# A fused transformer kernel: the NSA attention of the first mixer stepped by head pair instead of by token tile

## The chip, the cores and the metric

One NeuronCore of a Trainium2 chip runs the whole program. The metric is device time in microseconds (us) from launch to end, as the median of several executions. One further execution was profiled; its span and its rows are used below.

## The reference

Two transformer layers on 256 tokens of width 1024. The first layer's mixer is what the change touches. It has eight NSA query heads in two key/value groups (heads of 64), each with a compressed, a selected and a windowed branch; with 256 tokens, all blocks are selected and the window covers everything, so both of the latter branches are plain causal attention. Beside them run four slots of dilated attention.

```python
def masked_softmax(s, mask):
    s = jnp.where(mask, s, NEG_INF)
    return jax.nn.softmax(s, axis=-1) * mask
...
        ps = masked_softmax(ss, kpos <= t[:, None])
        o_s = jnp.einsum('bghtm,bgtmd->btghd', ps.astype(vs.dtype), vs)
...
        pw = masked_softmax(sw, wmask)
        o_w = jnp.einsum('bghtk,bkgd->btghd', pw.astype(vw.dtype), vw)
        o = gt[..., 0:1] * o_c + gt[..., 1:2] * o_s + gt[..., 2:3] * o_w
...
def reference(x, norm_g, even_w_in, ...):
    h = x
    for layer in range(DEPTH):
        y = rmsnorm(h, norm_g[layer, 0])
        y = even_mixer(...) if layer % 2 == 0 else odd_mixer(...)
        h = h + rmsnorm(y, norm_g[layer, 1])
        y = conv_ffn(rmsnorm(h, norm_g[layer, 2]), ...)
        h = h + rmsnorm(y, norm_g[layer, 3])
    return h
```

## The kernel before

Each engine runs a stream that was written out by hand, and semaphores tie the streams together. The attention of the first mixer stands between its input projection (`in0`) and its output projection (`out0`). It is a list of 16 items, `ITEMS`. Items 0 to 7 are dilated: one head slot and one token tile each, with 512 score columns. Items 8 to 15 are NSA: `("nsa", j, t)` is the head pair j (one head of each group) and the token tile t. The even items have t = 1 and see 256 keys ("wide", 4 x 256 score columns, for two heads times two branches); the odd ones have t = 0 and see 128 keys ("narrow", 4 x 128). Items 8 and 9 are one head pair, 10 and 11 the next.

An item n goes through these steps:

1. TensorE: scores (`dil_qk` or `nsa_qk`, two groups of matmuls, the second adds the mask; signals `it_scores`).
2. VectorE: negated row maxima (`it_maxima`, signals `it_max`).
3. ScalarE: the exponentials with their sums (`it_probs`; one activation for a dilated item, four for an NSA item; signals `it_exp`).
4. VectorE: reciprocals of the sums (`it_coefs`), then the probabilities times the coefficient (`it_scale`, signals `it_scaled`). For an NSA item a small product with the gates lies between.
5. TensorE: turns the scaled probabilities with transposes (`it_turn`, four of 128x128, eight for a wide item; signals `it_turned`).
6. ScalarE copies the first 512 turned columns to SBUF (`it_turned_out`, signals `it_pT0`); VectorE copies the other 512 of a wide item (`it_pT1`).
7. TensorE: the product with the values (`dil_values`, `nsa_values`, signals `it_pv`). When both token tiles of a head pair are in, ScalarE and VectorE split the output into a high and a low part (`tile_hi`, `tile_lo`) as operands of `out0`.

Banks of PSUM hold the scores (0 to 3; an even NSA item has banks 0 and 1, an odd one banks 2 and 3), the turned probabilities (4, and 5 for the second half of a wide item) and the outputs (6 and 7 in turn, by tile). `nsa_qk(n)` waits for the exponentials of item n - 2 (`it_exp`), whose scores lie in its banks. `probs` and `probsT` have three buffers each. The loops on the engines are skewed: in step n, TensorE issues the scores of n + 2, turns n, and multiplies the values of n - 1; ScalarE copies out the turned n and then does the exponentials of n + 2; VectorE takes the maxima of n + 2 and scales n + 1. The last NSA values are mixed with the first blocks of `out0` (`out_blocks`). The weights of that stage's last unit are split in halves (`SPLIT_AT`).

Of the kernel before, what the change touches and what calls it, by code (L numbers as in the profile page):

```python
# [15 lines left out]
F32 = mybir.dt.float32  # L16
# [64 lines left out]
def build(nc, x, weights, wgate, cmpw2, pe2, gpre, gpost, convw, rope, ropec, cmask, rows, masks, gcol, tri,  # L81
          out):
    ctx = ExitStack()
    with ctx:
# [89 lines left out]
        psh = ps[:, :, :].rearrange("p b (q c) -> p (b q) c", c=SEQ)  # L174

# [99 lines left out]
        TILE_OUT = {5: 0, 9: 1, 11: 2, 13: 3, 15: 4}  # L275
# [10 lines left out]
        def s_half(n):  # L286

            return 4 * (n % 2)
# [65 lines left out]
        def coefs_until(n):  # L354
            return sum(1 if kind == "dil" else 2 for kind, _, _ in ITEMS[:n + 1])
# [44 lines left out]
        def _(act):  # L400
# [125 lines left out]
            def it_probs(n):  # L526
                kind, _, t = ITEMS[n]
                s, w, o, v = n % 3, P * (t + 1), s_half(n), n % 4
# [6 lines left out]
                else:  # L535
                    for m in range(4):
                        act.activation(probs[:, s, m * w:(m + 1) * w], psh[:, o + m, 0:w], ACT.Exp,
                                       bias=stat[:, v, m:m + 1], accum_out=stat[:, v, 4 + m:5 + m]).then_inc(it_exp, 1)

            def it_turned_out(n):  # L540
# [4 lines left out]
                act.copy(probsT[:, n % 3, 0:BLK], ps[:, 4, :]).then_inc(it_pT0, 1)  # L545

            def tile_hi(tile):
                act.wait_ge(it_pv, TILE_DONE[tile])
                if tile < NSA0:
                    act.copy(xhi[:, tile, :].rearrange("p (i r) -> p i r", r=RES),  # L550
                             in_order(ps[:, 6 + tile % 2, 0:SEQ])).then_inc(ot_hi, 1)
                else:
                    act.copy(xhi[:, tile, :], ps[:, 6 + tile % 2, 0:SEQ]).then_inc(ot_hi, 1)
# [72 lines left out]
            for n in range(NI + 2):  # L626
                if n == 2:
                    act.wait_ge(unit_used, EVEN_END["unit", 6])
                    act.wait_ge(residue_rstd, 16 * TT * RES)
                    values_out(V_DIL + 256, 6, 0, BLK, True)  # L630
                if n < NI:
                    it_turned_out(n)
                if n in TILE_OUT:
                    tile_hi(TILE_OUT[n])
                if n + 2 < NI:
                    it_probs(n + 2)
                if n == NI:
                    tile_hi(NT - 1)
                if n in SPLIT_AT:
                    k = SPLIT_AT.index(n)  # L640
                    split_half(FIRST_UNIT["out0"] + LOOK + k // 2, k % 2)
# [133 lines left out]
        def _(dve):  # L775
# [285 lines left out]
            def it_maxima(n):  # L1061
                kind, _, t = ITEMS[n]
                s, w, o = n % 4, P * (t + 1), s_half(n)
                dve.wait_ge(it_scores, n + 1)
                if kind == "dil":
                    dve.tensor_reduce(stat[:, s, 0:1], ps[:, n % 4, :], AX.X, ALU.max, negate=True).then_inc(it_max, 1)
                else:
                    dve.tensor_reduce(stat[:, s, 0:4], psh[:, o:o + 4, 0:w], AX.X, ALU.max,
# [1010 lines left out]
```

## Time and profile before

| | |
|---|---|
| median of 3 executions | 657.6 us (657.31 to 657.97) |
| span of the profiled execution | 655.8 us |
| TensorE matmul busy | 646.6 us (99%) |
| VectorE busy | 460.1 us (70%) |
| ScalarE busy | 385.1 us (59%) |
| granted TensorE clock, mean | 1.000 |
| chain that ended last | TensorE 93%, VectorE 2%, GpSimd 2%, ScalarE 1% |

The span runs from the first to the last instruction of the profiled execution; the device time has about 1.8 us more around it. Busy shares are over the whole program, of which the attention items are some 45 us (98 to 148 us). Matmuls overlap in their pipeline, so the start of a group of instructions to the start of the next is what a group takes, and not its own duration. L numbers are lines of the kernel before.

### The profile page before, as it was taken

Reading aid. Unit: us, or ns where it says so; the run is one execution under the profiler, and the core shown is the slowest. Engines: PE = TensorE matmul, PEld = TensorE weight load, DVE = VectorE, ACT = ScalarE, POOL = GpSimd, SP = SyncE. Lnnn points to the kernel's source line nnn. Section 1 sums busy time; section 2 is a strip of 40 time slices with the busy share of each in tenths; the row PEclk is TensorE's granted clock in tenths of the full one; section 3 lists DMA queues with packets and bytes.
Section 4 is the critical chain, followed back from the end, with each engine's and each line's share of the span. In section 5 each row is a group of like instructions: output and inputs, shape, how many; then the busy total and the mean of one; then the engine's idle time right before and its main releaser. Section 6 shows DMA issues by size and latency. Waiting matters only on the chain.

```text
span 655.8 us, 9975 instructions
## 1 busy us (share of the span) xinstructions
PE 646.6 (99%) x3572; PEld 539.4 (82%) x3574; DVE 460.1 (70%) x627; ACT 385.1 (59%) x561; POOL 163.8 (25%) x123
## 2 busy tenths in 40 slices
PE   9999999999999999999999999999999999999996
PEld 6888887577888888888888888777888888888885
DVE  6498766877697878786457645676688788886532
ACT  7556355865757667666335535765567676767330
POOL 0323300001053444441001000680123434343000
PEclk9999999999999999999999999999999999999999
DMA  8987633004456363637652663304255554544601
GB/s 350 339 296 284 228 129 129 1 6 189 132 198 245 133 249 131 236 149 268 242 196 69 253 240 144 129 1 192 97 184 200 182 202 168 216 151 177 248 1 64
DMA packets 18971, 115.60 MB, mean 176 GB/s; under 512 B 2911, under 2 KB 3453, under 8 KB 6013
## 3 DMA queue, kind: packets, MB, share of 16 engines
q1 hardware_dynamic: 17789, 111.52, 45.7%
q10 hardware_dynamic: 1152, 3.67, 1.7%
q8 instruction: 20, 0.33, 0.2%
q14 instruction: 10, 0.08, 0.0%
HBM read 114.14 MB, written 1.05 MB: 176 GB/s over the span
## 4 chain that ended last, share of the span: by engine, by line
PE 93%; DVE 2%; POOL 2%; ACT 1%; issue 1%; DVEq 0%; POOLq 0%
PE ps L1423 27%; PE ps L1430 14%; PE ps L1380 11%; PE ps L1381 11%; PE ps L1382 11%; PE ps L1452 5%; PE ps L1507 2%; POOL sb_splo L1352 1%; PE ps L1751 1%; PE ps L1635 1%; PE ps L1371 1%; PE ps L1901 1%; PE ps L1679 1%; PE ps L1601 1%; PE ps L1738 1%
## 5 line engine op out<-in xcount | busy, mean ns | idle before, releaser
L778 DVE TENSOR_TENSOR wlo<-raw,whi 128x2048 fp32r<-128x2048 f32 x99 | 227.0, 2325 | 72.7 <-ACT whi L413 72.6
L413 ACT CAST whi<-raw 128x2048 fp32r<-128x2048 f32 x99 | 185.7, 1916 | 48.6 <-PE ps L1382 42.0
L1423 PE MATMUL ps<-xpair,whi 128*128 128x512 f32 x768 | 183.4, 391 | 0.0
L1423 PEld LDWEIGHTS ps<-xpair,whi 128*128 128x128 f32 x768 | 141.2, 188 | 27.6
L1430 PEld LDWEIGHTS ps<-xpair,wlo 128*128 128x128 f32 x768 | 98.5, 191 | 3.7
L1430 PE MATMUL ps<-xpair,wlo 128*128 128x256 f32 x768 | 99.6, 283 | 0.0
L1328 POOL TENSOR_TENSOR hidf<-act_g,conv 128x512 f32<-128x512 f32 x22 | 76.1, 3460 | 85.0 <-ACT act_g L671 85.0
L1380 PE MATMUL ps<-whi,hid_hi 128*128 128x512 f32 x176 | 68.5, 389 | 0.0
L1381 PE MATMUL ps<-wlo,hid_hi 128*128 128x512 f32 x176 | 68.5, 389 | 0.0
L1382 PE MATMUL ps<-whi,hid_lo 128*128 128x512 f32 x176 | 68.5, 389 | 0.0
L1380 PE MATMUL ps<-whi,xpair 128*128 128x512 f32 x168 | 67.7, 403 | 0.0
L1382 PE MATMUL ps<-whi,xpair 128*128 128x512 f32 x168 | 65.7, 391 | 0.0
L1381 PE MATMUL ps<-wlo,xpair 128*128 128x512 f32 x168 | 65.6, 390 | 0.0
L1282 POOL TENSOR_TENSOR rstd<-ms,mhalf 128x1 f32<-128x1 f32 x16 | 8.8, 551 | 212.0 <-DVE ms L842 179.1
L659 ACT COPY xn<-ps 128x512 f32<-128x512 f32 x40 | 21.5, 590 | 61.5 <-PE ps L1430 61.5
L1171 DVE SCALAR_TENSOR_TENSOR conv<-ps,c_conv,conv 128x255 f32<-128x255 f32 x88 | 38.2, 478 | 17.0 <-ACT conv L665 16.8
L665 ACT ACTIVATE conv<-ps,c_conv 128x256 f32<-128x256 f32 x88 | 42.6, 566 | 9.8 <-DVE ps L1160 9.8
L1330 POOL TENSOR_TENSOR hid_lo<-hidf,hid_hi 128x512 f32 (+1 forms) x22 | 28.7, 1304 | 74.7 <-ACT hid_hi L675 74.7
L1160 DVE TENSOR_TENSOR ps<-ps,xn 128x512 f32<-128x512 f32 x40 | 25.9, 694 | 24.6 <-ACT xn L659 24.6
L1382 PEld LDWEIGHTS ps<-whi,hid_lo 128*128 128x128 f32 x176 | 33.0, 188 | 6.9
L1380 PEld LDWEIGHTS ps<-whi,hid_hi 128*128 128x128 f32 x176 | 33.0, 188 | 6.8
L1381 PEld LDWEIGHTS ps<-wlo,hid_hi 128*128 128x128 f32 x176 | 33.1, 188 | 6.7
(197 smaller groups left out, 788.2 us busy)
## 6 DMA issues: line engine op xcount, KB each, us to landing
raw<-in_weights SPq DMA_DIRECT2D x101, 1024.0 KB, 5.0
c_gpost<-in_gpost ACTq DMA_DIRECT2D x4, 512.0 KB, 5.0
raw<-in_weights SPq DMA_DIRECT2D x3, 512.0 KB, 6.8
c_gpre<-in_gpre ACTq DMA_DIRECT2D x3, 512.0 KB, 4.3
h<-in_x SPq DMA_DIRECT2D x2, 512.0 KB, 3.8
out<-h SPq DMA_DIRECT2D x4, 256.0 KB, 2.0
raw<-in_weights SPq DMA_DIRECT2D x2, 256.0 KB, 4.8
t<-in_masks SPq DMA_DIRECT2D x1, 512.0 KB, 12.1
```

The costliest lines, as they stand in the source:

```text
L413: act.copy(whi[:, slot, :], raw[:, slot, :]).then_inc(hi_done, 1)
L665: act.activation(conv[:, par, m, :], ps[:, b0 + m, 0:SEQ], ACT.Identity, scale=c_conv[:, bass.ds(cofs + (4 * m + 2), 1)], bias=c_conv[:, b ...
L778: dve.tensor_tensor(wlo[:, slot, :], raw[:, slot, :], whi[:, slot, :].bitcast(F32), ALU.subtract).then_inc(lo_done, 1)
L1171: ins = dve.scalar_tensor_tensor(conv[:, par, m, 1:SEQ], ps[:, b0 + m, 0:SEQ - 1], c_conv[:, bass.ds(cofs + (4 * m + 1), 1)], conv[:, par, ...
L1328: pool.tensor_tensor(hidf[:, par], act_g[:, par], conv[:, par, 2:4, :], ALU.mult).then_inc(up_hf, 1)
L1330: pool.tensor_tensor(hid_lo[:, tile, :], hidf[:, par], hid_hi[:, tile, :].bitcast(F32), ALU.subtract).then_inc(up_lo, 1)
L1380: pe.matmul(out, s_hi, m_hi, start=start, stop=False, skip_group_check=shared)
L1381: pe.matmul(out, s_hi, m_lo, start=False, stop=False, skip_group_check=shared)
L1382: return pe.matmul(out, s_lo, m_hi, start=False, stop=stop, skip_group_check=shared)
L1423: pe.matmul(ps[:, b0 + m, :], whi[:, slot, cols], xpair[:, kt].rearrange("p a c -> p (a c)"), start=kt == 0, stop=kt == KT - 1, skip_group ...
L1430: ins = pe.matmul(ps[:, b0 + m, 0:SEQ], wlo[:, slot, cols], xhi[:, kt, :], start=False, stop=kt == KT - 1, skip_group_check=True)
L1452: ins = pe.matmul(ps[:, bank + t, :], x[:, kt, t * P:(t + 1) * P], w[:, u % RING, b * BLK:(b + 1) * BLK], start=kt == 0 and x is xhi and w ...
```

## The change

The items stay what they are, and so do their matmuls. What changes:

- In the loops of all three engines, items go by twos (n, n + 1), for NSA items both token tiles of a head pair. TensorE issues the scores of n + 2 and n + 3, turns n and n + 1, then multiplies the values of n - 2 and n - 1. ScalarE does the exponentials of n + 2 and n + 3 and then copies out n and n + 1. VectorE takes the maxima of n + 2 and n + 3, copies the second half of the turned n, then scales n + 2 and n + 3.
- The turned probabilities of a pair go to two banks (4 and 7), so that `it_turn(n)` waits for the copy of n - 2 instead of that of n - 1. All outputs go to bank 6, so that the first values of a tile wait for the low part of the tile just before (`ot_lo`), not of the one before that.
- Narrow scores lie in one bank for each group (256 columns side by side).
- The scaling of an NSA item takes two scalars (the reciprocal and the gate) in one instruction, and the small product of the two is left out.
- At the end TensorE turns item 14, multiplies the values of 12 and 13, turns 15, does two blocks of `out0`, multiplies the values of 14 and 15, and goes on with `out0`.

```diff
-        TILE_OUT = {5: 0, 9: 1, 11: 2, 13: 3, 15: 4}
+        TILE_OUT = {4: 0, ND: 1, ND + 2: 2, ND + 4: 3}
...
+        def turn_bank(n):
+
+            kind, _, t = ITEMS[n]
+            return 7 if (kind == "dil" and n >= 3 and n % 2 == 1) or (kind == "nsa" and t == 0) else 4
...
+            for n in range(2, NI - 2, 2):
+                it_probs(n + 2)
+                it_probs(n + 3)
+                it_turned_out(n)
+                it_turned_out(n + 1)
+                if n in TILE_OUT:
+                    tile_hi(TILE_OUT[n])
...
-                dve.wait_ge(it_coef, coefs_until(n) - 1)
-                gv = gates[:, t, :].rearrange("p (g i b) -> p g i b", g=2, b=BRANCH)[:, :, j, 1:3]
-                dve.tensor_tensor(coef[:, v, 4:8].rearrange("p (g b) -> p g b", g=2),
-                                  coef[:, v, 0:4].rearrange("p (g b) -> p g b", g=2), gv, ALU.mult).then_inc(it_coef, 1)
...
                 for m in range(4):
+                    gate = BRANCH * (NSA_PER * (m // 2) + j) + 1 + m % 2
                     ins = dve.tensor_scalar(probs[:, s, m * w:(m + 1) * w], probs[:, s, m * w:(m + 1) * w],
-                                            coef[:, v, 4 + m:5 + m], None, ALU.mult)
+                                            coef[:, v, m:m + 1], gates[:, t, gate:gate + 1], ALU.mult, ALU.mult)
...
+            for n in range(0, NI - 2, 2):
+                it_maxima(n + 2)
+                it_maxima(n + 3)
+                it_turned_out(n)
+                for e in range(2):
+                    it_coefs(n + 2 + e)
+                    it_scale(n + 2 + e)
...
                 if n in TILE_OUT:
                     tile_lo(TILE_OUT[n])
...
             def it_turn(n):
                 pe.wait_ge(it_scaled, n + 1)
-                if n >= 1:
+                if 1 <= n <= 2:
                     pe.wait_ge(it_pT0, n)
+                elif n == 3:
+                    pe.wait_ge(in_free_act, EVEN_ACT)
+                elif n >= 4:
+                    pe.wait_ge(it_pT0, n - 1)
...
-                if t == TT - 1 and tile >= 2:
-                    pe.wait_ge(ot_lo, tile - 1)
-                return ps[:, 6 + tile % 2, t * P:(t + 1) * P]
+                if t == TT - 1 and tile >= 1:
+                    pe.wait_ge(ot_lo, tile)
+                return ps[:, 6, t * P:(t + 1) * P]
...
-            for n in range(ND, NI - 1):
-                if n + 2 < NI:
-                    nsa_qk(n + 2)
-                if n == NI - 2:
-                    nsa_values(n - 1)
+            for n in range(ND, NI - 2, 2):
+                nsa_qk(n + 2)
+                nsa_qk(n + 3)
                 it_turn(n)
+                it_turn(n + 1)
                 if n == ND:
                     dil_values(ND - 2)
-                elif n < NI - 2:
+                else:
+                    nsa_values(n - 2)
                     nsa_values(n - 1)
+            it_turn(NI - 2)
+            nsa_values(NI - 4)
+            nsa_values(NI - 3)
+            it_turn(NI - 1)
```

A round of TensorE in the NSA items, before. The rows are the scores of item 12 (`qkT`, 128x512) with their mask, the turning of item 10 (`probs`), the values of 9 (`probsT`), the scores of 13 and the turning of 11:

```order
L1617 MATMUL ps<-qkT 128x512 [waits it_exp]
L1617 MATMUL ps<-qkT 128x512
L1621 MATMUL ps<-c_mask,c_identb 128x2x128 x2
L1635 MATMUL ps<-c_identf,probs 128x128 [waits it_pT1,it_pT0,it_scaled]
L1635 MATMUL ps<-c_identf,probs 128x128 x7
L1679 MATMUL ps<-probsT,vbuf 64x128 [waits it_pT1,it_pT0]
L1679 MATMUL ps<-probsT,vbuf 64x128 x3
L1617 MATMUL ps<-qkT 128x2x128 [waits it_exp]
L1617 MATMUL ps<-qkT 128x2x128
L1621 MATMUL ps<-c_mask,c_identb 128x2x128 x2
L1635 MATMUL ps<-c_identf,probs 128x128 [waits it_pT0,it_scaled]
L1635 MATMUL ps<-c_identf,probs 128x128 x3
```

The same place in the changed kernel (its line numbers are its own):

```order
L1626 MATMUL ps<-qkT 128x512 [waits it_exp]
L1626 MATMUL ps<-qkT 128x512
L1630 MATMUL ps<-c_mask,c_identb 128x2x128 x2
L1626 MATMUL ps<-qkT 128x256 [waits it_exp]
L1626 MATMUL ps<-qkT 128x256
L1630 MATMUL ps<-c_mask,c_identb 128x256 x2
L1648 MATMUL ps<-c_identf,probs 128x128 [waits it_pT1,it_pT0,it_scaled]
L1648 MATMUL ps<-c_identf,probs 128x128 x7
L1648 MATMUL ps<-c_identf,probs 128x128 [waits it_pT0,it_scaled]
L1648 MATMUL ps<-c_identf,probs 128x128 x3
L1686 MATMUL ps<-pcT,vc 128x256 [waits it_ot_lo,it_pT1,it_pT0]
L1692 MATMUL ps<-probsT,vbuf 64x128 x8
```

The scores of the narrow item have moved up to those of the wide one, and the values come behind both turnings.

ScalarE in the same rounds, before: the copy of the turned item 10, the exponentials of 12 (L537, 128x256), the copy of 11, the high part of a tile (`xpair`), the exponentials of 13, and the copy of 12:

```order
L545 COPY probsT<-ps 128x512 [waits it_pv,it_turned]
L537 ACTIVATE probs,stat<-ps,stat 128x256 [waits it_turned,it_max]
L537 ACTIVATE probs,stat<-ps,stat 128x256 x3
L545 COPY probsT<-ps 128x512 [waits it_pv,it_turned]
L553 CAST xpair<-ps 128x256 [waits it_pv]
L537 ACTIVATE probs,stat<-ps,stat 128x128 [waits it_turned,it_max]
L537 ACTIVATE probs,stat<-ps,stat 128x128 x3
L545 COPY probsT<-ps 128x512 [waits it_pv,it_turned]
```

In the changed kernel, the exponentials of 12 and 13, the copies of 10 and 11 and the high part of a tile, then the exponentials of 14:

```order
L540 ACTIVATE probs,stat<-ps,stat 128x256 [waits it_turned,it_max]
L540 ACTIVATE probs,stat<-ps,stat 128x256 x3
L540 ACTIVATE probs,stat<-ps,stat 128x128 [waits it_turned,it_max]
L540 ACTIVATE probs,stat<-ps,stat 128x128 x3
L548 COPY probsT<-ps 128x512 [waits it_pv,it_turned] x2
L556 CAST xpair<-ps 128x256 [waits it_pv]
L540 ACTIVATE probs,stat<-ps,stat 128x256 [waits it_turned,it_max]
```

The copies have moved from ahead of each item's exponentials to behind those of both.

The end of the NSA items on TensorE, before. The rows are the values of 12 and 13, the turning of 14 and the first block of `out0` (`xpair`), behind whose six matmuls the turning of 15 and the values of 14 follow:

```order
L1673 MATMUL ps<-pcT,vc 128x256 [waits it_ot_lo,it_pT1,it_pT0]
L1679 MATMUL ps<-probsT,vbuf 64x128 x8
L1679 MATMUL ps<-probsT,vbuf 64x128 [waits it_pT1,it_pT0]
L1679 MATMUL ps<-probsT,vbuf 64x128 x3
L1635 MATMUL ps<-c_identf,probs 128x128 [waits it_pT1,it_pT0,it_scaled]
L1635 MATMUL ps<-c_identf,probs 128x128 x7
L1380 MATMUL ps<-whi,xpair 128x512 [waits it_ot_lo,lo_done,it_exp]
```

In the changed kernel:

```order
L1692 MATMUL ps<-probsT,vbuf 64x128 [waits it_pT1,it_pT0]
L1692 MATMUL ps<-probsT,vbuf 64x128 x3
L1648 MATMUL ps<-c_identf,probs 128x128 [waits it_pT1,it_pT0,it_scaled]
L1648 MATMUL ps<-c_identf,probs 128x128 x7
L1686 MATMUL ps<-pcT,vc 128x256 [waits it_ot_lo,it_pT1,it_pT0]
L1692 MATMUL ps<-probsT,vbuf 64x128 x8
L1692 MATMUL ps<-probsT,vbuf 64x128 [waits it_pT1,it_pT0]
L1692 MATMUL ps<-probsT,vbuf 64x128 x3
L1648 MATMUL ps<-c_identf,probs 128x128 [waits it_pT0,it_scaled]
L1648 MATMUL ps<-c_identf,probs 128x128 x3
L1385 MATMUL ps<-whi,xpair 128x512 [waits it_ot_lo,lo_done,it_exp]
```

Here the first row is the end of the values of 11, then comes the turning of 14, and the values of 12 and 13 stand behind it.

## Rows read from the trace of the kernel before

**Rows 1.** The page: busy share of TensorE, and its granted clock.

```profile
PE 646.6 (99%) x3572; PEld 539.4 (82%) x3574; DVE 460.1 (70%) x627; ACT 385.1 (59%) x561; POOL 163.8 (25%) x123
PEclk9999999999999999999999999999999999999999
```

**Rows 2.** Waits of TensorE's matmuls from 150 us on: total, times, longest.

```profile
PE ps L1901 <- POOL sb_splo L1352: 1.1, 2, 0.6
```

**Rows 3.** Timeline of TensorE, items 8 to 10: start, duration, what, [idle before].

```profile
116.02 1.13 PE L1617 MATMUL ps<-qkT 64*128 64x512 f32 x4
...
120.76 1.13 PE L1617 MATMUL ps<-qkT 64*128 64x512 f32 x4 [0.43 <-ACT probs L537]
...
122.34 1.09 PE L1635 MATMUL ps<-c_identf,probs 128*128 128x128 f32 x8
```

**Rows 4.** Timeline of TensorE, one pair period.

```profile
127.24 1.13 PE L1617 MATMUL ps<-qkT 64*128 64x512 f32 x4
...
128.53 1.04 PE L1635 MATMUL ps<-c_identf,probs 128*128 128x128 f32 x8
129.50 0.66 PE L1679 MATMUL ps<-probsT,vbuf 128*64 128x128 f32 x8
130.09 0.70 PE L1617 MATMUL ps<-qkT 64*128 64x256 f32 x4
130.72 0.39 PE L1621 MATMUL ps<-c_mask,c_identb 128*128 128x256 bf16 x2
131.20 0.66 PE L1635 MATMUL ps<-c_identf,probs 128*128 128x128 f32 x4
131.85 0.67 PE L1673 MATMUL ps<-pcT,vc 128*128 128x256 f32 x2
...
133.47 1.13 PE L1617 MATMUL ps<-qkT 64*128 64x512 f32 x4
```

**Rows 5.** Timeline of ScalarE, items 10 to 13.

```profile
130.09 0.48 ACT L537 ACTIVATE probs<-ps,stat 128x256 f32<-128x256 f32 x1
...
131.81 0.22 ACT L537 ACTIVATION_READ_ACCUMULATOR probs<-ps,stat 128x1 f32 x1
131.90 0.61 ACT L545 COPY probsT<-ps 128x512 f32<-128x512 f32 x1
132.38 0.40 ACT L553 CAST xpair<-ps 128x256 fp32r<-128x256 f32 x1
132.64 0.41 ACT L537 ACTIVATE probs<-ps,stat 128x128 f32<-128x128 f32 x1
...
133.94 0.26 ACT L537 ACTIVATION_READ_ACCUMULATOR probs<-ps,stat 128x1 f32 x1
135.84 0.59 ACT L545 COPY probsT<-ps 128x512 f32<-128x512 f32 x1 [1.65 <-PE ps L1635]
```

**Rows 6.** Timeline of VectorE, items 8 and 11 to 14.

```profile
117.52 1.22 DVE L1068 TENSOR_REDUCE stat<-ps 128x4 f32<-128x1024 f32 x1
...
128.74 1.22 DVE L1068 TENSOR_REDUCE stat<-ps 128x4 f32<-128x1024 f32 x1 [0.79 <-PE ps L1621]
129.88 0.17 DVE L1089 RECIPROCAL coef<-stat 128x4 f32<-128x4 f32 x1
...
130.28 0.87 DVE L1105 TENSOR_SCALAR probs<-probs,coef 128x128 f32<-128x128 f32 x4
...
132.67 1.14 DVE L1105 TENSOR_SCALAR probs<-probs,coef 128x256 f32<-128x256 f32 x4
133.72 0.42 DVE L1117 TENSOR_TENSOR xpair<-ps,xpair 128x256 fp32r<-128x256 f32 x1
134.97 1.22 DVE L1068 TENSOR_REDUCE stat<-ps 128x4 f32<-128x1024 f32 x1 [0.83 <-PE ps L1621]
```

**Rows 7.** Timeline of TensorE: the turning of item 14, the first row behind the last values.

```profile
140.14 1.09 PE L1635 MATMUL ps<-c_identf,probs 128*128 128x128 f32 x8
...
147.99 0.50 PE L1380 MATMUL ps<-whi,xpair 128*128 128x512 f32 x1
```

More of the change, by code:

```diff
@@ L354, in coefs_until @@
         def coefs_until(n):
-            return sum(1 if kind == "dil" else 2 for kind, _, _ in ITEMS[:n + 1])
+            return n + 1
         block = ctx.enter_context(nc.Block())
@@ L623, in _ @@
                     it_probs(1)
[L626 to L630, printed above, removed]
+            it_turned_out(0)
+            it_probs(2)
+            it_probs(3)
+            it_turned_out(1)
+            act.wait_ge(unit_used, EVEN_END["unit", 6])
+            act.wait_ge(residue_rstd, 16 * TT * RES)
+            values_out(V_DIL + 256, 6, 0, BLK, True)
+            for n in range(2, NI - 2, 2):
[5 more added lines that the diff above has]
+                    tile_hi(TILE_OUT[n])
+            for n in range(NI - 2, NI + 2):
                 if n < NI:
                     it_turned_out(n)
-                if n in TILE_OUT:
-                    tile_hi(TILE_OUT[n])
-                if n + 2 < NI:
[L636 to L641, printed above, removed]
+                if n >= NI - 1 and n - (NI - 1) < 2:
+                    tile_hi(NT - 2 + n - (NI - 1))
+                k = SPLIT_AT.index(n)
+                split_half(FIRST_UNIT["out0"] + LOOK + k // 2, k % 2)
             plain_stage("out0", 2)
@@ L1116, in tile_lo @@
                 else:
-                    dve.tensor_tensor(xlo[:, tile, :], ps[:, 6 + tile % 2, 0:SEQ], xhi[:, tile, :].bitcast(F32),
+                    dve.tensor_tensor(xlo[:, tile, :], ps[:, 6, 0:SEQ], xhi[:, tile, :].bitcast(F32),
                                       ALU.subtract).then_inc(ot_lo, 1)
@@ L1139, in _ @@
                     tile_lo(TILE_OUT[n])
-                if n == NI:
-                    tile_lo(NT - 1)
-                if n in SPLIT_AT:
-                    k = SPLIT_AT.index(n)
-                    split_half(FIRST_UNIT["out0"] + LOOK + k // 2, k % 2)
+            for n in range(NI - 2, NI + 2):
+                if n < NI:
+                    it_turned_out(n)
+                if n >= NI - 1 and n - (NI - 1) < 2:
+                    tile_lo(NT - 2 + n - (NI - 1))
+                k = SPLIT_AT.index(n)
+                split_half(FIRST_UNIT["out0"] + LOOK + k // 2, k % 2)
             def plain_stage(name, ahead=0):
```

77 lines of the change are left out of this document (32 added, 45 removed).

## The prediction

> **What bounds the kernel now.** I read the page first: TensorE is busy 99% of the span and the clock was granted in full in all forty slices [rows 1]. Then its waits behind the attention: from 150 us to the end matmuls waited 1.1 us in all [rows 2]. So what comes behind the attention is a solid run of matmuls, and a microsecond won or lost before it arrives whole at the end. The profiled span of 655.8 us with some 1.8 us around it is the 657.6 us of the median. A difference of 0.2%, 1.3 us, is about what a measurement of this kernel can tell from no change.
>
> Inside the attention I read the start of a group to the start of the next. A pair of NSA items takes 6.23 us (127.24 to 133.47) [rows 4]. Its work: wide scores with mask 1.29 (to 128.53), turning a wide item 0.97 (to 129.50), narrow values 0.59 (to 130.09), narrow scores 0.63 and mask about 0.23, turning a narrow item about 0.5, wide values with the compressed part about 1.55. That is 5.76 us. The rest is a wait: the turning at 131.20 should have come at 130.95, took 0.65 and not 0.5, and the next group 1.62. So 0.47 us are lost, here and once more in the next pair: 0.94 us. Ahead of them the scores of item 10 start at 120.76, where TensorE had been free at about 120.26: 0.5 us, and the turning of item 8 at 122.34 instead of 122.05: 0.3 us [rows 3]. That turning took 1.03 and not 0.97. Together **1.8 us of waits before**. No version can win more than that here, because the change leaves every matmul of TensorE as it is.
>
> **What the change removes and adds.** From VectorE it takes eight small products with the gates, 0.2 us each with their wait (the reciprocal at 129.88, the scaling at 130.28, the product between) [rows 6]. VectorE isn't the engine waited for at the point where they stood, as the next part shows, so they are worth little. Outputs, bank of the narrow scores, number of transposes and copies: no price of their own. All the rest is order, so I laid the new order out by hand: each group starts when its engine is free and its waits are over (0.04 us later; a TensorE that had waited takes 0.1 more), with the durations of the rows. The same layout of the old order ends within 0.1 us of the trace at 147.99 [rows 7].
>
> **The new loop through ScalarE and VectorE.** In a round, VectorE takes the wide maxima; ScalarE can start the wide exponentials 1.25 later (1.22 and a semaphore) [rows 6]; they take 1.81 (130.09 to 131.90), the narrow ones 1.38 (132.64 to 133.94 and 0.09 to the next), two copies 0.48 each, and the cast of the tile's high part is done 0.41 after its start [rows 5]. Only then may VectorE subtract the low part (0.42, the next may start after 0.34), and only behind that stand, in its order, the next wide maxima. The sum is 1.25 + 1.81 + 1.38 + 0.96 + 0.41 + 0.34 = **6.15 us a round**, whatever TensorE does. TensorE's work for a round is 5.76. The old order had the copies and maxima interleaved and ran 6.23 with the wait. So the pair step swaps one loop for another of the same length, and wins almost nothing in the steady state.
>
> **Where TensorE waits then.** Until 116.02 the dilated rounds have slack in both orders; no wait arises, and the scores of item 8 start there as before [rows 3].
> - TensorE then does both scores, both turnings and dilated values: 116.02 + 1.29 + 0.86 + 0.5 + 0.5 + 1.03, free at 120.2 (120.0 in the closest layout). VectorE gets to the wide maxima of item 8 at 117.65 (117.52 before [rows 6]), because the low part of tile 0 is ahead. The exponentials of 8 run from 118.90 to 120.85 (1.94 with the last read of the sum [rows 5]). The scores of item 10 wait for them and start at 120.99. Wait: 1.0.
> - The narrow exponentials of 9 are done at 122.2; VectorE scales it (0.2 and 0.79 [rows 6]) and reaches the maxima of 10 at 123.24. From here the loop sets the pace: maxima of 12 at 129.40, of 14 at 135.56, where the trace has 128.74 and 134.97 [rows 6].
> - Exponentials of 10 are done at 126.44. TensorE was free at 125.62 and starts the scores of 12 at 126.58. Wait: 1.0. Those of 12 are done at 132.60: free 132.30, start 132.74. Wait: 0.4.
> - TensorE ends the values of 11 at 138.46. Next in its queue is the turning of item 14. It wants item 14 scaled (about 140.1) and bank 4 free, which is ScalarE's copy of the turned item 12. That copy was at 135.84 in the old order [rows 5]; now it stands behind the exponentials of 14 and 15: 135.56 + 1.25 + 1.81 + 1.38 = 140.0, done at 140.59. The turning starts at 140.73 (140.14 before [rows 7]). **Wait: 2.3**, and nothing else can be issued, since the values of 12 and 13 and the blocks of `out0` are queued behind it.
> - The values of 12 then want bank 6 free, that is the low part of tile 3: cast at 140.96, low part done at 141.80. TensorE is there at 141.70 and starts at 141.94. Wait: 0.2. Before, the values of 12 and 13 were already done when item 14 was turned.
>
> The sum is 1.0 + 1.0 + 0.4 + 2.3 + 0.2 = 4.9 us of waits after, less 1.8 to 1.9 before: **3.0 us more**. The splits of the next weights move by only 1.5 us, so they don't add. 657.6 + 3.0 = **660.6 us**.
>
> **The disputed price: scaling with two scalars.** No row before has such an instruction on this size. The nearest from below is the same one with a single scalar, four of 128x256 in 1.14 us, four of 128x128 in 0.87; from above, the elementwise subtraction of 128x256 with 0.42 a piece [rows 6]. Laid out at the subtraction's pace (0.3 us more for four), the loop gets longer and the total is 1.1 us more. Nothing excludes a gain, but if it were 0.2 us faster the total moves by only 0.1, since the exponentials end last there. I take the one-scalar price, as it is the same instruction on the same buffers.
> The Trainium skill (VectorE: DVE Perf Modes, "The perf-mode tier table") has fp32 `tensor_scalar` in SBUF at two elements a cycle and `tensor_tensor` at one, and a second [P, 1] scalar isn't a second tensor; by it the price stays. The rows for one scalar agree with the faster tier.
>
> **The rivals.**
> - *The scaling loses its pace* (above): 657.6 + 3.0 + 1.1 = 661.7 us. For it: a second operand is read. Against: no second stream of elements. Chance 0.12.
> - *The clock falls in the long wait.* Before, TensorE never waited over 0.5 us in the attention, and the granted clock stayed at the upper level of 2.4 GHz [rows 1, 3]. Two waits of 1 us and one of 2.3 us are new. If it fell to 1.2 GHz, each group behind would take up to twice as long; on 3 us of such groups this is 3 us more: 663.6 us. Chance 0.08.
>   The Trainium skill (TensorE: Matmul & The Clock Gate, "What's actually happening") says that recent activity of the array sets the clock and that half rate is its idle state. No run here shows yet what this wait does.
> - *Faster, the other side.* The pairing does what a reader would hope: ScalarE and VectorE run both tiles of a pair without waits between, and are ahead. Then the 1.8 us are won: 655.8 us. It needs one thing: the exponentials of item n done before TensorE comes to the scores of n + 2, at 125.6 instead of 126.44, so a first round of VectorE (117.65 to 123.24) of 4.8 us instead of 5.6, and also item 12 copied by 138.5 instead of 140.59. Against it stands the sum of 6.15 us from rows. Chance 0.05.
> - *No change to be told.* Part of the end's wait goes away, if the loop is entered earlier or its cross-engine steps are shorter by 0.15 us each: then the last wait is 1 us and the total 658.9 or less. Chance 0.1.
> - The forecast itself has 0.65.
>
> **How the numbers follow.** The likeliest is 660.6 us; its own error is that of the layout, about 0.7 us. Over all cases the range goes from 659.0 (part of the end's wait gone) to 662.8 (scaling slower and some clock lost); it leaves the faster case and most of the clock case out. Slower by over 0.2%: 0.65 + 0.12 + 0.08 and a little of the next, 0.86; within 0.2%: 0.09; faster: 0.05.
>
> **What would show it.** In the profile after: scores of items 10 and 12 waiting on the exponentials for 0.8 to 1.0 us; wide maxima 6.15 us apart, each right behind a low part; no idle time of ScalarE between the exponentials and the two copies; a gap on TensorE from 138.5 to 140.7 that ends with ScalarE's copy; four scalings of 128x256 in 1.1 to 1.2 us; the block row of 147.99 about 3 us later in the same work. The prediction is wrong if the maxima are under 5.8 us apart, if the turning of item 14 starts before 139.5, or if the clock shows less than full.

## The result, and the profile after

| | kernel before | changed kernel |
|---|---|---|
| median of 4 executions each, in turn on one chip | 657.49 us (657.31 to 657.97) | 661.83 us (661.03 to 662.47) |
| ratio | | 1.0066, 95% interval 1.0054 to 1.0077 |
| span of the profiled execution | 655.8 us | 659.2 us |
| mean granted clock | 1.000 (the profiled execution) | 0.997 (the profiled one), and three of 0.995 |

The change costs 4.3 us; 660.6 us (659.0 to 662.8) was predicted. The profiled execution of the changed kernel, with 661.03 us, is its fastest; its span is 3.4 us above that of before.

The page (the busy times), which answers to [rows 1]:

```profile
PE 645.7 (98%) x3574; PEld 539.9 (82%) x3574; DVE 460.6 (70%) x619; ACT 384.8 (58%) x561; POOL 163.8 (25%) x123
PEclk9999999999999999999999999999999999999998
```

TensorE's work is the same (two of its records are missing in the page of before). VectorE has eight instructions less (the products) and is busy 0.5 us longer. TensorE's waits, over the whole trace (waited for, total, times, longest):

```profile
PE ps L1648 <- ACT probsT L548: 2.6, 1, 2.6
PE ps L1626 <- ACT probs L540: 2.6, 3, 1.2
...
PE ps L1913 <- POOL sb_splo L1357: 1.1, 2, 0.6
PE ps L1686 <- DVE xpair L1121: 0.3, 1, 0.3
```

L1913 is the only one behind 150 us, as in [rows 2]. The other three shown lie in the attention. TensorE's timeline there, which answers to [rows 3, 4, 7]:

```profile
115.99 1.13 PE L1626 MATMUL ps<-qkT 64*128 64x512 f32 x4
...
121.00 1.13 PE L1626 MATMUL ps<-qkT 64*128 64x512 f32 x4 [0.70 <-ACT probs L540]
...
126.97 1.13 PE L1626 MATMUL ps<-qkT 64*128 64x512 f32 x4 [1.20 <-ACT probs L540]
...
133.26 1.13 PE L1626 MATMUL ps<-qkT 64*128 64x512 f32 x4 [0.67 <-ACT probs L540]
...
141.48 1.07 PE L1648 MATMUL ps<-c_identf,probs 128*128 128x128 f32 x8 [2.59 <-ACT probsT L548]
142.86 0.67 PE L1686 MATMUL ps<-pcT,vc 128*128 128x256 f32 x2 [0.31 <-DVE xpair L1121]
143.46 1.53 PE L1692 MATMUL ps<-probsT,vbuf 128*64 128x128 f32 x24
144.92 0.66 PE L1648 MATMUL ps<-c_identf,probs 128*128 128x128 f32 x4
...
151.66 0.40 PE L1385 MATMUL ps<-whi,xpair 128*128 128x512 f32 x1
```

The waits are those of the prediction, at the same places and for the same work: 0.70, 1.20 and 0.67 us for the exponentials, 2.59 for the copy of the turned item 12, 0.31 for the low part of tile 3. Their sum is 5.47 us. Less the 1.8 of before that is 3.67 us. The last row is the 19th matmul of `out0`, as is the row of 147.99 in [rows 7] (both have all of the attention in front of them): 3.67 us later. That both differences come to 3.67 is in part chance, as the 1.8 is a rounded sum. Of the 3.67 us, 3.4 arrive in the span: from this matmul to the end it is 507.5 us, and 507.8 before. What makes the 0.3 us was not looked for.

A round of VectorE and the start of the next, which answers to [rows 6]:

```profile
130.03 1.21 DVE L1076 TENSOR_REDUCE stat<-ps 128x4 f32<-128x1024 f32 x1
...
133.24 0.18 DVE L1096 RECIPROCAL coef<-stat 128x4 f32<-128x4 f32 x1 [0.81 <-ACT probs L540]
133.46 1.38 DVE L1109 TENSOR_SCALAR probs<-probs,coef,gates 128x256 f32<-128x256 f32 x4
134.75 0.17 DVE L1096 RECIPROCAL coef<-stat 128x4 f32<-128x4 f32 x1
134.97 1.12 DVE L1109 TENSOR_SCALAR probs<-probs,coef,gates 128x128 f32<-128x128 f32 x4
135.99 0.42 DVE L1121 TENSOR_TENSOR xpair<-ps,xpair 128x256 fp32r<-128x256 f32 x1
136.33 1.21 DVE L1076 TENSOR_REDUCE stat<-ps 128x4 f32<-128x1024 f32 x1
```

And ScalarE in that round:

```profile
131.28 0.47 ACT L540 ACTIVATE probs<-ps,stat 128x256 f32<-128x256 f32 x1 [1.73 <-DVE stat L1076]
...
135.41 0.44 ACT L556 CAST xpair<-ps 128x256 fp32r<-128x256 f32 x1
```

Two things differ from the prediction. The maxima are 6.30 us apart, not 6.15. And from 133.24 on VectorE has no idle time: the cast of the high part is done at 135.85, while VectorE scales the narrow item to 135.99. The loop closes on VectorE itself, with one stretch on ScalarE in it. From start to start: maxima 1.25, wide exponentials 1.96 (131.28 to 133.24), then its own reciprocal and wide scaling 1.51, narrow ones 1.24, low part 0.34, which makes 6.30. Four scalings with two scalars take 1.38 and 1.12 us where one scalar took 1.14 and 0.87.

The clock stayed at its upper level in the attention of this execution. In the slower ones the mean clock is 0.995; that this is more than an accompaniment is shown below.

### The profile page after: what moved, and what is told of

Read it like the earlier page. It is cut to its first block, busy times and chain, and to the rows that moved or that the text cites. A ratio compares the mean times of both kernels' runs of the same rounds, so it can differ in the third digit from the quotient of the medians.

```text
span 659.2 us, 9968 instructions
## 1 busy us (share of the span) xinstructions
PE 645.7 (98%) x3574; PEld 539.9 (82%) x3574; DVE 460.6 (70%) x619; ACT 384.8 (58%) x561; POOL 163.8 (25%) x123
## 3 DMA queue, kind: packets, MB, share of 16 engines
q10 hardware_dynamic: 1152, 3.67, 1.7%
## 4 chain that ended last, share of the span: by engine, by line
PE 90%; DVE 4%; ACT 2%; issue 2%; POOL 2%; DVEq 0%; POOLq 0%; ACTq 0%
PE ps L1428 27%; PE ps L1435 14%; PE ps L1385 11%; PE ps L1386 11%; PE ps L1387 11%; PE ps L1457 5%; PE ps L1512 2%; DVE probs L1109 1%; POOL sb_splo L1357 1%; PE ps L1764 1%; PE ps L1376 1%; DVE stat L1076 1%; PE ps L1913 1%; ACT probs L540 1%; PE ps L1606 1%
```

## The experiments

Each was timed in turn with the kernel before, the kernels built from the changed one with five executions (the early copy with four), those built from the kernel before and the one with both cuts with eleven (medians of before in the three groups of runs: 657.49, 657.53 and 657.43 us). The traces differ by up to 0.8 us in when the attention begins, so within it times are counted from the scores of item 8 (115.99 in the changed kernel, 116.02 before). "Period" is the distance of the wide maxima of items 12 and 14. "One" exponential or scaling means one instruction for all four heads and branches of an item; those four kernels compute something else than the reference.

| kernel | us | lowest to highest | ratio to before | period |
|---|---|---|---|---|
| changed kernel again | 661.76 | 660.69 to 662.16 | 1.0063 [1.0049, 1.0076] | 6.29 |
| product and one scalar | 661.83 | 661.33 to 661.95 | 1.0064 [1.0050, 1.0078] | 6.21 |
| low parts behind the maxima | 659.94 | 659.90 to 660.32 | 1.0039 [1.0026, 1.0053] | 5.95 |
| before, with two scalars | 657.59 | 657.12 to 658.11 | 1.0002 [0.9993, 1.0011] | 6.28 |
| matmuls in the last wait | 660.66 | 660.19 to 660.98 | 1.0046 [1.0033, 1.0060] | 6.29 |
| one narrow exponential | 662.12 | 660.93 to 662.32 | 1.0065 [1.0051, 1.0079] | 6.30 |
| one scaling | 660.90 | 659.83 to 661.82 | 1.0050 [1.0036, 1.0063] | 6.19 |
| one scaling and one exponential | 657.03 | 656.60 to 657.34 | 0.9993 [0.9984, 1.0002] | 5.46 |
| before, with the same two cuts | 656.64 | 656.12 to 656.83 | 0.9985 [0.9976, 0.9994] | 5.84 |
| copy of 12 early | 663.77 | 662.95 to 664.03 | 1.0094 [1.0079, 1.0109] | 6.30 |
| low parts later, and matmuls | 660.87 | 660.79 to 661.21 | 1.0054 [1.0040, 1.0068] | 5.98 |
| before, item 11 scaled first | 657.01 | 656.53 to 657.87 | 0.9996 [0.9987, 1.0005] | 5.04 |

**The changed kernel again**, unaltered.

> The changed kernel once more, unaltered, to see how far its single executions lie apart (four gave 661.03 to 662.47 us with spans of 659.2 to 660.7, while those of before lay within 0.7 us). If the extra 1.3 us over the forecast of 660.6 is the price of the scaling, the profile shows again a span of about 659.2 to 659.5, wide maxima 6.30 us apart and a median of 661 to 662. If a part of it is a clock that falls in some executions, single executions scatter by over 1 us and a profile shows a granted clock under 1.00 somewhere ahead of the last matmul.

Its five executions: 660.97 and 660.69 us at a mean clock of 1.000, 661.76 at 0.997, 661.86 and 662.16 at 0.995. With the four of the result: at 0.998 or more 660.7 to 661.0 us, at 0.995 661.5 to 662.5, at 0.997 one of each kind (661.03, whose trace has the clock lowered only behind 655 us, where no matmul runs, and 661.76). The kernel before, of which 51 executions were timed beside these kernels, was under 0.998 in two: 0.997 at 657.85 us, and 0.947 at 658.50, its slowest. So 3.2 to 3.5 us of the loss are there at full clock, and the rest comes with a lower one, in six of the nine executions. Both profiled executions of this kernel are among the three at full clock: no trace of it shows the clock falling, and for the other six only the mean clock tells it.

**Product and one scalar.** The scaling of before, in the changed order.

```diff
+                dve.tensor_tensor(coef[:, v, 4:8]..., coef[:, v, 0:4]..., gv, ALU.mult).then_inc(it_coef, 1)
...
-                                            coef[:, v, m:m + 1], gates[:, t, gate:gate + 1], ALU.mult, ALU.mult)
+                                            coef[:, v, 4 + m:5 + m], None, ALU.mult)
```

> The changed kernel with the scaling of before: the small product with the gates is back and each scaling takes one scalar. Theory A (the two-scalar instruction costs 0.24 us more for four, and the product that it saves gives 0.20 back, so the form of the scaling is nearly neutral and the order carries the loss): four scalings in 1.14 and 0.87 us again, wide maxima 6.2 us apart, about 0.4 us faster than the changed kernel, 661.4 or so. Theory B (the forecast was right on the order at 660.6 and the form of the scaling is what made it 661.8): 1.2 us faster, 660.6.

**Before, with two scalars.** The same swap the other way round, in the kernel before.

> The kernel before with only the form of the scaling changed (two scalars, no product). Theory A: four scalings take 1.38 and 1.11 us, the product's 0.20 us is saved, the turnings of items 11 and 13 come 0.05 us later: 0.1 to 0.2 us slower than before, not to be told from it. Theory B (the form alone carries over 1 us): 658.5 or more.

Neither moves the median. The second scalar costs 0.24 us on four instructions, 0.06 on each, and the product costs 0.20 with its wait: nearly a swap of equals. The profiled execution of the first of these kernels shows the clock falling. Windows of a microsecond (start and end, length, busy time and instructions of five engines, then the granted clock, the share of the DMA engines, GB/s):

```profile
142.00:143.00 1.00, 0.87 (x2) 0.50 (x2) 0.63 (x1) 1.00 (x2) 0.00 (x0) 0.50 0.00 0
143.00:144.00 1.00, 1.00 (x9) 0.76 (x10) 0.50 (x1) 0.47 (x1) 0.00 (x0) 0.50 0.00 0
144.00:145.00 1.00, 1.00 (x12) 1.00 (x10) 0.73 (x1) 0.00 (x0) 0.00 (x0) 0.50 0.07 16
145.00:146.00 1.00, 1.00 (x15) 0.83 (x12) 0.00 (x0) 0.00 (x0) 0.00 (x0) 0.85 0.00 0
146.00:147.00 1.00, 1.00 (x8) 0.87 (x7) 0.00 (x0) 0.61 (x2) 0.00 (x0) 1.00 0.00 0
```

Its TensorE timeline in them:

```profile
140.84 1.07 PE L1655 MATMUL ps<-c_identf,probs 128*128 128x128 f32 x8 [2.50 <-ACT probsT L548]
142.13 1.19 PE L1693 MATMUL ps<-pcT,vc 128*128 128x256 f32 x2 [0.22 <-DVE xpair L1128]
143.25 2.52 PE L1699 MATMUL ps<-probsT,vbuf 128*64 128x128 f32 x24
145.69 0.66 PE L1655 MATMUL ps<-c_identf,probs 128*128 128x128 f32 x4
```

Right behind the long wait and the eight transposes the clock is at its lower level (0.50, that is 1.2 GHz), from shortly before 142 to about 145.3, for about 3.4 us. The values of 12 and 13 take 3.56 us (142.13 to 145.69) and not 2.06 (142.86 to 144.92): 1.5 us lost. The Trainium skill (TensorE: Matmul & The Clock Gate, "What's actually happening") has the lower rate as the state of an array that has not been busy; the rows of 0.50 behind the wait agree. The wait alone doesn't settle it: both traces of the changed kernel have 1.00 behind a wait as long. The order alone was 0.3 us better here (turning of item 14 at 25.23 us from the scores of 8, against 25.49), which the clock hid: this kernel had 0.995 in all five executions. Among the executions at 0.995 alone the medians are 661.83 us and, for the changed kernel, 662.16.

**Matmuls in the last wait.** Ten bf16 matmuls of 128x512 without use, into a bank that is free, ahead of the turning of 14. Nothing that is computed changes.

```diff
+            pe.wait_ge(it_pT1, wide_before(NI - 2))
+            for _ in range(10):
+                pe.matmul(ps[:, 5, :], c_identb[:], c_mask[:, 0:2, :]..., start=True, stop=True, ...)
             it_turn(NI - 2)
```

> The changed kernel with ten matmuls of identity by mask (128x512 in bf16, about 2.1 us, written to bank 5 and overwritten by the turning) ahead of the turning of item 14, in the time in which TensorE waits 2.6 us anyway. Clock theory (in most executions the wait lets the clock fall to half for some 3 us, as the profile of the one-scalar run shows from 142 to 145 us, and this costs 1.0 to 1.5 us): the granted clock stays 1.00 through the attention in every execution, the median is 660.7 to 661.0 and the single executions lie within 0.5 us. Rival (the scatter has another cause, such as the transfers of weights that start then): median and scatter stay at 661.8 and 1.5 us.

```profile
139.01 2.10 PE L1839 MATMUL ps<-c_mask,c_identb 128*128 128x512 bf16 x9 [0.16 <-issue]
141.43 1.06 PE L1648 MATMUL ps<-c_identf,probs 128*128 128x128 f32 x8 [0.32 <-DVE probs L1109]
```

(One of the ten has no record in the trace.) The turning starts as late as in the changed kernel (25.48 us from the scores of 8, against 25.49), and the clock is at 1.00 in every window of the attention. No execution is above 660.98 us, and the median is 1.1 us lower; the single executions lie within 0.8 us, where 0.5 was expected. The clock, then, is a cause and not a companion. By this kernel it is 1.1 us of the changed kernel's median; by the changed kernel's own three executions at full clock (median 660.97) it is 0.8 to 0.9.

**Which chain paces the loop.** Four kernels shorten one chain or the other. The first takes ScalarE's four narrow exponentials together, with one row maximum and one sum.

```diff
+                elif t == 0:
+                    act.activation(probs[:, s, 0:BLK]..., ps[:, 2:4, 0:2 * P], ACT.Exp,
+                                   bias=stat[:, v, 0:1], accum_out=stat[:, v, 4:5]).then_inc(it_exp, 4)
...
```

> The changed kernel with one exponential of 512 columns for a narrow item instead of four of 128 (all four heads share the first one's maximum and sum, so the result isn't the reference's). It takes 0.7 us from ScalarE in each round and leaves VectorE's work as it is. Loop through VectorE (maxima 1.25, wide exponentials 1.97, wide scaling 1.51, narrow scaling 1.24, low part 0.34, 6.30 us in all): wide maxima stay 6.3 us apart and the time stays at 661 to 662. Loop through ScalarE, as the forecast had it (1.25 + 1.81 + 1.38 + 0.96 + 0.41 + 0.34): it would fall to 5.5, TensorE would set the pace, and the time would be 2 us or more shorter.

```profile
129.80 1.22 DVE L1079 TENSOR_REDUCE stat<-ps 128x4 f32<-128x1024 f32 x1
...
136.10 1.21 DVE L1079 TENSOR_REDUCE stat<-ps 128x4 f32<-128x1024 f32 x1
```

The maxima stay 6.30 us apart and the time is that of the changed kernel. The prediction's chain, in which these exponentials were a term, does not set the pace.

The next one has one scaling for each NSA item in place of four.

```diff
-                for m in range(4):
...
+                ins = dve.tensor_scalar(probs[:, s, 0:4 * w], probs[:, s, 0:4 * w],
+                                        coef[:, v, 0:1], gates[:, t, gate:gate + 1], ALU.mult, ALU.mult)
```

> The changed kernel with one scaling instruction for each NSA item (the whole row by one coefficient and one gate) in place of four; the result is another function than the reference's. If VectorE's chain (maxima, wide exponentials, reciprocal, both scalings, low part) sets the loop, the wide maxima come 5.6 to 5.9 us apart (6.30 in the changed kernel), the waits for exponentials shrink to under 1.5 us in all, and TensorE's order is 1.2 to 1.6 us earlier at the end: 659.3 to 660.6 us, the upper value if the clock still falls in the last wait. If ScalarE's chain of the prediction (6.15 us) set it, the maxima would stay 6.1 us or more apart and the time be 661.3 us or more. With the kernel of a single exponential for the narrow item (6.30 apart) and that with both cuts (5.46 apart) this gives each cut alone and both together.

It gains 0.9 us, less than VectorE's chain promises, and VectorE's timeline says why:

```profile
125.74 0.81 DVE L1108 TENSOR_SCALAR probs<-probs,coef,gates 128x1024 f32<-128x1024 f32 x1
126.92 0.18 DVE L1096 RECIPROCAL coef<-stat 128x4 f32<-128x4 f32 x1 [0.37 <-ACT probs L540]
127.14 0.55 DVE L1108 TENSOR_SCALAR probs<-probs,coef,gates 128x512 f32<-128x512 f32 x1
128.16 0.42 DVE L1115 TENSOR_TENSOR xpair<-ps,xpair 128x256 fp32r<-128x256 f32 x1 [0.48 <-ACT xpair L553]
128.50 1.21 DVE L1076 TENSOR_REDUCE stat<-ps 128x4 f32<-128x1024 f32 x1
```

Now VectorE idles 0.48 us for ScalarE's cast, which stands behind the narrow exponentials and both copies. That is the chain of the prediction; it was summed to 6.15 us and measures 6.19. It was there all along, hidden behind one 0.1 us longer. The expectation had put the loop at 5.6 to 5.9 us (VectorE's) or 6.1 and more with no gain (ScalarE's); the truth took the period of the second and, through the first round (5.29 us, where no low part stands), part of the gain of the first. The lower clock is in this trace too, and in three of the five executions (0.995 and 0.996); the two others took 659.8 us.

With both cuts:

> As the run before, and one scaling for an NSA item instead of four (all four heads take the first one's coefficient and gate). Both legs of the loop get shorter: the maxima come 5.5 us apart, under the 5.76 of TensorE's work, and the wait ahead of the turning of item 14 shrinks from 2.6 to about 0.5 us. Loop theory: 3.7 us faster than the changed kernel at full clock, and no execution loses its clock: about 657.3. Rival (the pair order costs what it costs by the bank that the turned item 12 holds, or by the end's order, whatever the pace): the wait ahead of item 14 stays over 1.5 us, and at most 1.5 us are won.

The period falls to 5.46 us. TensorE's waits:

```profile
PE ps L1651 <- DVE probs L1112: 1.0, 1, 1.0
PE ps L1629 <- ACT probs L543: 0.7, 1, 0.7
```

One cut gives nothing, the other 0.9 us, both 4.7 us: two chains of 6.30 and 6.19 us have to be cut together. Of the 4.7 us, 3.7 are order (the first block row behind the values of 14 stands at 30.52 us from the scores of 8, not at 34.18), and the rest is the clock: at 657.03 us the longest wait in the attention is 1.0 us, and the mean clock was never under 0.997.

The kernel before with the same two cuts:

> The same two cuts in the kernel before (its small product stays). There TensorE sets the pace already, and only its waits for the scaling of items 8, 11 and 13 can go (0.3 + 2 x 0.47 us): 1.0 to 1.3 us faster than before, 656.3, where the pair order wins over 4 us by the same cuts. If the cuts win as much here as there, their gain says nothing of the order.

It is 0.9 us faster than the kernel before (1.0 to 1.3 was expected), and still 0.4 us faster than the pair step with the same cuts, though it keeps its products; in the traces its 19th matmul of `out0` comes 1.2 us earlier (30.83 us from the scores of 8, against 32.01). With these cuts the pair step's loop of 5.46 us is shorter than TensorE's work of 5.76, and TensorE still waits 1.9 us, in the first round and at the end. So even there the new order wins nothing.

**Low parts behind the maxima.** VectorE's low parts of tiles 1 and 2 are moved behind the next pair's maxima.

```diff
+                if n >= ND + 2:
+                    tile_lo(TILE_OUT[n - 2])
...
-                if n in TILE_OUT:
+                if n < ND and n in TILE_OUT or n == NI - 4:
                     tile_lo(TILE_OUT[n])
```

> The changed kernel with the low part of tiles 1 and 2 moved on VectorE behind the maxima of the next pair. The loop theory (VectorE's own chain of maxima, exponentials, both scalings, low part sets the pace at 6.30 us): the wide maxima come 0.34 us closer, 5.97 us apart, the wait ahead of the turning of item 14 shrinks from 2.6 to about 1 us, but the values of item 8 now wait about 1 us for the low part of tile 1; in all 0.7 us faster than the changed kernel. The rival (the pace is TensorE's or ScalarE's): maxima stay 6.3 us apart and the time is the same or worse by the new wait.

The period falls by the low part's 0.34 us, to 5.95. The first block row behind the values of 14 stands at 33.47 us from the scores of 8, against 34.18: 0.7 us of order. The median fell by 1.8 us. The other 1.1 is the clock: the turning of 14 waits 0.73 us and not 2.59, and all executions are at 0.998 or 0.999. What was taken from the low part has a price: with all outputs in one bank, the values of item 8 now wait 1.3 us for the low part of tile 1 (L1116).

```profile
PE ps L1628 <- ACT probs L540: 1.9, 2, 1.2
...
PE ps L1688 <- DVE xpair L1116: 1.3, 1, 1.3
PE ps L1650 <- DVE probs L1109: 0.7, 1, 0.7
```

**Low parts later, and matmuls** in the wait, both edits together.

> The changed kernel with two edits together: the low parts of tiles 1 and 2 behind the next pair's maxima, and ten matmuls without use (they write an unused bank) in the wait ahead of the turning of item 14. The kernel with the first edit alone took 659.94 us at a mean clock of .998 to .999, with the second alone 660.66 us. If the first edit's 1.8 us were 0.7 of order and 1.1 of clock, the second edit has nothing left to give and the time is 659.7 to 660.3 us. If the two gains are independent, 658.9 us or less.

```profile
139.87 2.10 PE L1841 MATMUL ps<-c_mask,c_identb 128*128 128x512 bf16 x9 [0.16 <-issue]
141.82 1.04 PE L1650 MATMUL ps<-c_identf,probs 128*128 128x128 f32 x8
```

The same turning in the kernel with the low parts alone:

```profile
140.43 1.06 PE L1650 MATMUL ps<-c_identf,probs 128*128 128x128 f32 x8 [0.73 <-DVE probs L1109]
```

The gains are not independent. But 660.87 us also missed what was expected, by a term left out: the ten matmuls take 1.95 us (139.87 to 141.82), the wait that they fill is now only 0.73, and the turning of 14 starts 1.4 us later for them (both traces have the scores of 8 at the same time within 0.01 us). The values of 12, which no longer wait for the low part of tile 3, start 0.9 us later, and 0.9 us is what the median lost. With this term the case without independence gives 659.94 + 0.9, which was measured. In these two kernels the ten matmuls paid where the wait was 2.6 us long, and cost where it was 0.73.

**Copy of 12 early.** The prediction ended the long wait with ScalarE's copy of item 12. Here that copy stands ahead of the exponentials of 15.

```diff
                 it_probs(n + 2)
+                if n == NI - 4:
+                    it_turned_out(n)
                 it_probs(n + 3)
```

> The changed kernel with one line moved at the end of ScalarE's stream: the copy of the turned item 12 stands ahead of the exponentials of item 15, not behind them. The prediction ended the long wait ahead of the turning of item 14 with this copy. Theory A, that the scaling of item 14 on VectorE ends that wait almost as late as the copy does: the wait stays 2.2 to 2.5 us, its releaser in the trace becomes the scaling, item 15 is ready later, and the time is that of the changed kernel within 0.4 us (661.4 to 662.2 with the same clock). Theory B, that the copy's place costs the wait: the turning of 14 starts 1 us or more earlier and the time is 660.3 us or less.

```profile
140.84 1.09 PE L1651 MATMUL ps<-c_identf,probs 128*128 128x128 f32 x8 [2.30 <-DVE probs L1112]
142.88 1.19 PE L1689 MATMUL ps<-pcT,vc 128*128 128x256 f32 x2 [0.95 <-DVE xpair L1124]
144.00 2.83 PE L1695 MATMUL ps<-probsT,vbuf 128*64 128x128 f32 x24
146.76 1.12 PE L1651 MATMUL ps<-c_identf,probs 128*128 128x128 f32 x4
```

The window behind them (columns as above) has the granted clock at 0.50 throughout:

```profile
142.00:148.00 6.00, 5.12 (x31) 4.17 (x32) 2.56 (x5) 1.59 (x3) 0.00 (x0) 0.50 0.01 3
```

Theory A holds for the wait: it ends 0.3 us earlier, with VectorE's scaling of 14. The copy and the scaling end within 0.3 us of each other too. A failed for the time, 2.0 us above the changed kernel. Item 15 is ready later, with it the low part of tile 3 (0.95 us of wait and not 0.31), and between the two waits TensorE has one microsecond of work. The values of 12 and 13 start only 0.4 us later than in the changed kernel, but the turning of 15 behind them 2.2 us later: at the lower clock they take 3.88 us and not 2.06, and the clock stays low to the end of the window. The lower clock came in all four executions (0.994 to 0.996). The second wait, of 0.95 us at the lower clock, may be what keeps it down for longer here (6 us and more, against 3.4); no run tries that alone.

**Before, item 11 scaled first.** What is left to win in the kernel before: VectorE scales item 11 ahead of the maxima of 12.

```diff
+                early = n == ND + 2
+                if early:
+                    it_coefs(n + 1)
+                    it_scale(n + 1)
```

> The kernel before with one move on VectorE at the second NSA pair: the reciprocal and scaling of item 11 ahead of the maxima of item 12, instead of behind them. In the trace of before the turning of item 11 waits 0.25 us for that scaling and starts 0.4 us late in its effect. By a layout with the durations of the trace this gives 0.4 to 0.5 us: 657.0 to 657.2 us against 657.5 of the kernel before. The other theory: the later maxima of 12 delay its exponentials and the scores of 14 by as much as is won, and the time is 657.5 us or more.

```profile
126.73 1.13 PE L1621 MATMUL ps<-qkT 64*128 64x512 f32 x4
...
130.44 0.60 PE L1639 MATMUL ps<-c_identf,probs 128*128 128x128 f32 x4
...
132.43 1.13 PE L1621 MATMUL ps<-qkT 64*128 64x512 f32 x4
```

The pair takes 5.70 us, where [rows 4] have 6.23: the turning of 11 waits no more, and the scores of 14 don't either. The 19th matmul of `out0` comes 0.53 us earlier than before. The medians are 0.42 us apart, but the interval of the ratio holds 1. The period of 5.04 us in the table is no loop time: the move puts the maxima of 12 later and leaves those of 14. The gain in order is shown in the trace; in the time it is at the edge of what can be measured. This is the lowest median of a kernel that computes the same function.

## Why the prediction was right, and where it was not

**Right: TensorE's work is the same, so only its waits count.** 5.47 us of waits after, less 1.8 before, is some 3.7, and the same matmul of `out0` is 3.67 us later.

**Right: places and causes of the waits.** The five of the prediction are the five of the trace. Sizes: 0.70 for 1.0, 1.20 for 1.0, 0.67 for 0.4, 2.59 for 2.3, 0.31 for 0.2. The sum was 4.9 and is 5.5. In time, 660.6 us was forecast and the executions at full clock took 660.7 to 661.0. The median of 661.83 lies 1.2 us above the forecast, and the upper end of the range, 662.8, was given for what happened, "scaling slower and some clock lost".

**Wrong: "the new loop through ScalarE and VectorE".** The loop was given to ScalarE's exponentials, copies and cast, 6.15 us. That chain is real (6.19 when VectorE's scaling is cut), but the longer one is VectorE's own, 6.30. Taking 6.15 us of ScalarE's work as the pace cost the prediction little in time, and would have misled anyone who acted on it: the cut in ScalarE gave nothing.

**Mis-sized: the scaling with two scalars.** It was priced as with one. It costs 0.24 us more on four, near the upper bound of 0.3. The pace by the element was rightly taken as that of one scalar (512 more elements take 0.26 us with either); what the prediction had left out is a fixed price for each instruction. By the durations of before VectorE's chain would be about 0.5 us shorter, 5.8 us, and ScalarE's would have led. So this one price swapped the leading chain; that is worked out from durations, and no kernel ran with one scalar and no product. "VectorE isn't the engine waited for at the point where they stood" was the sentence that failed: in the changed order VectorE is waited for, and the products removed are worth the second scalar that replaces them. In the kernel before, too, the turning of 11 had waited for VectorE's scaling, as the kernel that scales 11 first shows. The rival "the scaling loses its pace" had the price; its 661.7 us agree with the median by accident, as the full-clock executions are at 660.7 to 661.0.

**Rival that came true in most executions: the clock.** It had a chance of 0.08 and 3 us. By the mean clock it fell in six of nine executions, and it costs 0.8 to 1.1 us of the median; where it is seen in a trace of another kernel, the values of 12 and 13 behind it lose 1.5 to 1.8 us. The size was too large because only some 2 us of work lie in it before the clock is back. Without it the changed kernel would be 3.1 to 3.5 us slower, with it 4.3. The prediction had named a clock at less than full as one of three signs of being wrong; that sign came, and the other two did not.

**Right against: the faster case.** It wanted a first round of VectorE of 4.8 us and expected 5.6; it took 5.96 (117.77 to 123.73), and with both cuts, 4.83 us. Even then the result was that of before, no better.

**Open.** What one bank for all outputs costs by itself was not tried alone; the trace gives 0.31 us in the changed kernel, and 1.3, 0.2 and 0.3 us once the low parts are moved. Nor was the end of the order tried alone: the turning of 14 stands ahead of the values of 12 and 13 and of the blocks of `out0`, so that nothing fills its wait of 2.6 us, nearly half of all waits. The kernel with both cuts shows only that this wait shrinks to 1.0 when the loop is shorter. Why the clock falls in some executions of one kernel and not in others, no run here tells.

## What to carry to other kernels

When an order is changed so that engines hand over larger pieces, sum the loop through each engine, its own instructions as well as the hand-overs; where two sums lie within 0.2 us of 6, a price of 0.06 us an instruction decides which one leads, and cutting either alone shows little. Fusing a small product into the instructions that use it is a gain only if the extra operand on all of them costs less than the product. A wait of TensorE of some 2.5 us had two prices here, itself and the clock behind it: look at the spread of the executions, and at the clock of each, before a median is explained by order alone.

## What the runs showed of the hardware that was not expected

- A second scalar of 128x1 on an fp32 scaling in SBUF costs VectorE the same whatever the size: 0.24 us on four of 128x256 (1.14 to 1.38) and on four of 128x128 (0.87 to 1.12), 0.06 on one of 128x1024 (0.75 to 0.81) and on one of 128x512 (0.49 to 0.55). It is a price for each instruction and not for each element: from 512 to 1024 columns both forms take 0.26 us more.
- Behind a wait of 2.3 to 2.5 us the clock was at its lower level for some 3.4 us in the traces of three kernels. By the mean clock of 0.995 this came in all five executions of one of them, and in most, not all, of the changed kernel, whose instructions of TensorE are the same and whose two traces have the clock up behind waits of 2.59 and 2.58 us. With ten matmuls without use in the wait the trace has it up, and no mean clock is under 0.997. Waits of up to 1.3 us, one in each round of some 6 us, left it up in every trace.
- The clock can make a small loss of order a large one of time: in the kernel with the early copy the last two waits are 0.4 us longer together, its trace has the lower clock for over 6 us, and the time is 2.0 us longer.
